# Block inverse on half the columns, and the scan's buffers moved so that the merge's first loads start inside its last chunks

## The chip, the cores and the metric

The kernel runs on one core of one Trainium2 chip. The metric is the device time of one execution in microseconds (us), taken as the median of the runs. All operands lie in HBM at the start, and the result is written back to it.

## The reference, cut to what matters

A residual block of width 1024 over 512 positions (and 256 positions of context) with three mixers side by side: an RWKV-7 scan, a convolution and a matrix LSTM. A gated merge, a projection and an MLP follow; then two layers of a second block, each with a feed-forward, a mixer made of a gated delta rule and two attentions, and another feed-forward. What the change touches is the RWKV scan, the delta rule and the merge:

```python
def step(S, inp):                      # RWKV-7, per position, 8 heads of 64, in both directions of time
    S = (S * w_t[:, :, None, :]
         - jnp.einsum('bhvk,bhk->bhv', S, kk_t)[..., None] * (kk_t * a_t)[:, :, None, :]
         + v_t[..., None] * k_t[:, :, None, :])
    y = jnp.einsum('bhvk,bhk->bhv', S, inp[5])

def _merge(u_gate, ya, yb, yc, pa, pb, pc, wo):
    ga, gb, gc = jnp.split(jax.nn.sigmoid(u_gate), N_BRANCH, axis=-1)
    m = ga * (ya @ pa) + gb * (yb @ pb) + gc * (yc @ pc)
    return m @ wo
```

`u_gate` is h @ w_in[:, OFF_GATE:], with h the normed input of the block. The delta rule of the second block has the same form of step.

## The kernel before, in words

**Engines and order.** Each engine has a program of its own, written out by hand in the order in which it runs (`tensor_program`, `vector_program`, `scalar_program`, `pool_program`, `sync_program`). An engine works strictly in that order and waits on semaphores: `K.at(name)` is the point at which a named result is done. `E.come(name)` marks how far an engine has got, `E.meet(name)` makes an engine wait for all marks of that name.

**Weights.** They come as slabs of 128x2048 fp32 (1 MB) into a ring of three slots, issued by the DMA queue of SP in `sync_program`. ACT copies a slab to a rounded form ("w hi", 128x2048), DVE subtracts to get the rest ("w lo"), and a product is three matmuls on the rounded parts (`mm3`, 128x512 each; one slab is 48 of them). `E.ahead()` is the place in the ACT and DVE programs at which the slabs up to the one after the current one are split, in order; `E.ahead_of(n)` splits up to the current slab plus n. `K.late[j]` names a mark that SP waits for before slab j is loaded.

**The scan** (`pe_rwkv` and its fellows). Time is cut into 6 tiles of 128 positions, each of two chunks of 64, for two directions d = 0, 1. Three streams per direction are interleaved in fixed turns by `rw_turns`: operands of a tile, the inverse of a tile, and the recurrence over the chunks; direction 1 runs five turns behind direction 0. The tile's triangular 64x64 blocks (8 heads, two chunks stacked on the partitions) are inverted by doubling, in `pe_invert`, `act_invert` and `dve_invert`: for n = 1 to 5 PE forms X = A T (16 matmuls 64x64, in fp32), ACT copies X to SBUF, PE forms the two products N of X with T and its transpose TT (32 matmuls; 16 for n = 5), and DVE takes over, with COPY_PREDICATED under the mask of level n, the half of the columns that this level changes (one instruction for TT, one for T, 128x512 each). In the profile an fp32 matmul is two records. There are 12 such inversions in the scan, and four per layer in the delta rule (`pe_prep`, `act_prep`, `dve_prep`, names `gd0`, `gd1`), so 8 there. Between the levels stands the rest of the scan's work on each engine. The first step (n = 0) works on 128x256 pieces (in the scan) or whole (in the delta rule).

**Memory.** The scan needs more room than the arena has: its buffers (`room` in `memory`) lie in the place of the block's input h (`m.hL`, spilled to `spill_h` before), in the ring of slabs, in a stretch of the arena from `mk2` on, and over part of the constants, all handed out in that order of places.

**From the scan to the merge.** After `E.meet("RWKV done")`, POOL (`pool_rw_out`) loads g2, two rows of norm parameters and h in two halves of 2 MB; SP loads slab 0 of the merge at once, and slabs 1 and 2 each after a half of h has landed (`K.merge_slab`). PE multiplies the gate by g2 (`pe_rw_out`, 4 fp32 matmuls 128x512), then takes slabs 0 and 1 (w_in for the first gate, with h), then slab 2 (p_c, with the split `yop`). DVE and ACT norm the scan's output in `dve_rw_out` and `act_rw_out`, with `E.ahead()` after the second of four tiles, and after the variance. ACT forms four sigmoids of the first gate, and then splits `ycT` to `yop`, which shares memory with what the norm reads, so that it waits for "rw out" 3, the end of the norm.

Of the kernel before, what the change touches and what calls it, by code (L numbers as in the profile page):

```python
# [17 lines left out]
SLOT = 2048  # L18
# [481 lines left out]
def sync_program(e, K):  # L500

    landed = [0] * NSLOT
    for j, (pieces, size, split) in enumerate(K.slabs):
# [3 lines left out]
        if j - K.merge_slab in (1, 2):  # L507
            e.wait_ge(*K.at("in", "hx", j - K.merge_slab - 1))
# [241 lines left out]
def memory(K):  # L750
# [89 lines left out]
    def room(n):  # L840
# [4 lines left out]
    m.Ya = m.ycT  # L845
    m.rsw = room(512)
    m.rw = [Names() for _ in range(2)]
    for d, s in enumerate(m.rw):
        s.SA, s.BK, s.UV = (room(1024) for _ in range(3))
        s.sets = [Names() for _ in range(2)]  # L850
        for z in s.sets:
            z.TK, z.MB, z.AK = (room(1024) for _ in range(3))
    for d, s in enumerate(m.rw):
        s.La, s.En, s.AT, s.T, s.X, s.Xs, s.St = (room(512) for _ in range(7))
        for z in s.sets:
            z.KKp, z.Rp, z.TT = (room(512) for _ in range(3))
            z.AT, z.T, z.X = s.AT, s.T, s.X
            z.edge = room(8)
        s.PCM = m.tmp[:, 512 * d:512 * d + 512]
# [1043 lines left out]
def pe_invert(t, K, st, s, key, ready):  # L1903

    for n in range(1, 6):
        o = t.take(st, "X", n, key)
        t.wait_ge(*(K.at(*ready) if n == 1 else K.at(st, "T", n - 1, key)))
        pe_blocks(t, (o, True, s.AT, s.T, (st, "X", n, key)))  # L1910
# [3 lines left out]
        both = [(o[0], False, s.X, s.TT, (st, "N", n, 0, key))]  # L1914
        if n < 5:
            both.append((o[1], True, s.TT, s.X, (st, "N", n, 1, key)))
        pe_blocks(t, *both)
# [3 lines left out]
def act_invert(a, K, st, s, key):  # L1921
# [14 lines left out]
def dve_invert(v, K, st, s, low, key):  # L1936
    for n in range(1, 6):
        m, mt = doubling(K, n, low)
        yield
        for j, (dst, msk) in enumerate([(s.TT, mt), (s.T, m)][:2 if n < 5 else 1]):  # L1940
# [2181 lines left out]
```

## Time and profile before

| | us |
|---|---|
| median of 3 runs (lowest to highest) | 4334.55 (4328.83 to 4341.07) |
| the profiled execution | 4335.74 |
| its span, first to last instruction | 4333.6 |
| mean granted clock of TensorE | 0.953 |
| PE busy | 4030.1 (93%) |
| DVE busy | 2159.5 (50%) |
| ACT busy | 1344.9 (31%) |

The stages that the change touches, in us from the span's start: the scan from about 530 to 966.6 (its last operands and inversions end near 935), the merge from 966.6 on, the delta rule of layer 0 from about 2180 to 2300 and of layer 1 from about 3504 to 3625. PE's clock is 1.0 at 2.4 GHz and 0.5 at 1.2 GHz. Busy shares are averages over stages with different limits, so each stage is read by itself. A matmul's record includes its way through the array: records overlap, and the spacing of a row of them is (time of the row less one record) / (count - 1).

### The profile page before, as it was taken

What the parts mean: (1) busy time and instruction counts of PE and PEld (TensorE: products, weight loads), DVE (VectorE), ACT (ScalarE), POOL (GpSimd) and SP (SyncE); (2) the same over time, 40 slices, a digit from 0 to 9 for tenths busy, and PEclk for the clock granted to TensorE, in tenths of its full rate; (3) what the DMA queues carried; (4) which work ended last, traced back from release to release, by engine and by line L of the source; (5) the groups of instructions that cost most, each with busy time, mean ns of one, the idle gap of its engine ahead of it and who ended that gap; (6) DMA issues with size and microseconds to landing.
All of it is one profiled execution on the core that took longest, in us unless ns stands there. A gap on an engine that the chain in (4) does not pass through costs nothing.

```text
span 4333.6 us, 70136 instructions
## 1 busy us (share of the span) xinstructions
PE 4030.1 (93%) x30330; PEld 3217.4 (74%) x30330; DVE 2159.5 (50%) x2941; ACT 1344.9 (31%) x1903; POOL 178.6 (4%) x214
## 2 busy tenths in 40 slices
PE   7998878888999999999988999999999988999998
PEld 5756768876767887888677578887888767578887
DVE  4866467754434445335665453345334755453335
ACT  4253233312324223222322532223222322433222
POOL 0000011211000000000010000000000001000000
PEclk9998879999999999999998899999999998999999
DMA  6212000004242223332102023332333101013331
GB/s 241 69 59 88 10 2 3 3 22 177 99 144 84 97 97 88 98 97 88 50 3 81 8 84 97 97 102 83 98 97 106 51 3 62 27 53 108 97 98 59
DMA packets 319781, 328.41 MB, mean 76 GB/s; under 512 B 10097, under 2 KB 243617, under 8 KB 318065
## 3 DMA queue, kind: packets, MB, share of 16 engines
q1 hardware_dynamic: 312144, 287.53, 21.4%
q0 software_dynamic: 7328, 36.40, 2.2%
q8 instruction: 239, 3.92, 0.4%
q14 instruction: 70, 0.57, 0.0%
HBM read 315.51 MB, written 8.39 MB: 75 GB/s over the span
## 4 chain that ended last, share of the span: by engine, by line
PE 80%; DVE 11%; ACT 4%; issue 3%; DMA 1%; POOL 0%; DVEq 0%; ACTq 0%; SPq 0%; POOLq 0%
PE psum L246 78%; DVE ring L300 2%; DVE ring L331 2%; DVE arena L300 2%; ACT ring L350 1%; PE psum L253 1%; ACT arena L350 1%; DVE arena L311 1%; DVE r L300 1%; ACT r L350 1%; DMA ring<-in_w_in 1%; DMA ring<-in_w_ada 0%; DVE arena L307 0%; DVE arena L331 0%; ACT L350 0%
## 5 line engine op out<-in xcount | busy, mean ns | idle before, releaser
L246 PE MATMUL psum<-r 128*128 128x512 f32 (+2 forms) x13008 | 2929.2, 387 | 68.9 <-DVE r L300 58.7
L246 PEld LDWEIGHTS psum<-r 128*128 128x128 f32 x13008 | 2369.7, 189 | 617.6 <-DVE r L300 53.0
L300 DVE TENSOR_TENSOR r<-ring,r 128x2048 fp32r<-128x2048 f32 (+2 forms) x261 | 575.7, 2206 | 385.3 <-ACT r L350 381.5
L350 ACT ACTIVATE r<-ring 128x2048 fp32r<-128x2048 f32 (+2 forms) x261 | 479.3, 1836 | 386.1 <-PE psum L246 325.7
L350 ACT ACTIVATE arena<-psum 128x512 f32<-128x512 f32 (+7 forms) x464 | 254.2, 548 | 1029.2 <-PE psum L246 949.0
L246 PE MATMUL psum<-arena 64*64 64x64 f32 (+15 forms) x2750 | 398.6, 318 | 39.9 <-DVE arena L300 23.1
L246 PE MATMUL psum<-ring 64*64 64x64 f32 (+4 forms) x8608 | 349.3, 234 | 82.3 <-ACT ring L350 35.6
L300 DVE TENSOR_TENSOR arena<-arena,psum 128x512 f32<-128x512 f32 (+4 forms) x224 | 132.6, 592 | 580.2 <-PE psum L246 560.9
L246 PEld LDWEIGHTS psum<-arena 64*64 64x64 f32 (+7 forms) x2750 | 252.4, 171 | 175.5 <-issue 118.1
L246 PEld LDWEIGHTS psum<-ring 64*64 64x64 f32 (+3 forms) x8608 | 287.4, 143 | 119.8 <-issue 46.7
L311 DVE SCALAR_TENSOR_TENSOR arena<-arena 128x512 f32<-128x512 f32 (+4 forms) x316 | 266.7, 844 | 117.9 <-ACT arena L350 106.8
L350 ACT ACTIVATE r<-arena 128x512 fp32r<-128x512 f32 (+1 forms) x176 | 109.4, 622 | 517.8 <-DVE arena L300 515.8
L350 ACT ACTIVATE ring<-psum 128x512 f32<-128x512 f32 (+5 forms) x262 | 140.4, 536 | 399.8 <-PE psum L246 330.0
L246 PE MATMUL psum<-ring,arena 64*64 64x64 f32 (+5 forms) x2408 | 195.8, 306 | 43.5 <-DVE ring L300 11.8
L300 DVE TENSOR_TENSOR arena<-arena 128x512 f32<-128x512 f32 (+6 forms) x298 | 183.2, 616 | 91.1 <-ACT arena L350 79.7
L246 PE MATMUL psum<-arena,ring 64*64 64x64 f32 (+4 forms) x2784 | 190.3, 258 | 16.9 <-ACT ring L350 7.1
L300 DVE TENSOR_TENSOR r<-arena,r 128x512 fp32r<-128x512 f32 (+1 forms) x176 | 119.8, 681 | 150.8 <-ACT r L350 148.1
L246 PEld LDWEIGHTS psum<-ring,arena 64*64 64x64 f32 (+4 forms) x2408 | 126.0, 150 | 88.9 <-issue 34.5
L246 PEld LDWEIGHTS psum<-arena,ring 64*64 64x64 f32 (+3 forms) x2784 | 153.0, 161 | 48.9 <-issue 30.6
L350 ACT ACTIVATE arena<-arena 128x512 f32<-128x512 f32 (+10 forms) x186 | 80.9, 435 | 334.2 <-DVE arena L307 158.3
L331 DVE COPY_PREDICATED ring<-arena,psum 128x512 f32<-128x512 uint32 (+1 forms) x202 | 136.1, 680 | 39.4 <-PE psum L246 29.9
L300 DVE TENSOR_TENSOR arena<-psum,arena 128x512 f32<-128x512 f32 (+5 forms) x107 | 70.4, 658 | 157.9 <-PE psum L246 97.5
(93 smaller groups left out, 1382.9 us busy)
## 6 DMA issues: line engine op xcount, KB each, us to landing
ring<-in_ffa_w_in SPq DMA_DIRECT2D x88, 512.0 KB, 5.1
ring<-in_ffb_w_in SPq DMA_DIRECT2D x88, 512.0 KB, 5.1
ring<-in_w_mlp SPq DMA_DIRECT2D x32, 1024.0 KB, 5.3
ring<-in_w_in SPq DMA_DIRECT2D x31, 1024.0 KB, 5.4
ring<-in_w_ada SPq DMA_DIRECT2D x24, 1024.0 KB, 5.4
ring<-in_mix_w_in SPq DMA_DIRECT2D x24, 1024.0 KB, 5.2
ring<-in_ffa_w_out SPq DMA_DIRECT2D x20, 1024.0 KB, 5.0
ring<-in_ffb_w_out SPq DMA_DIRECT2D x20, 1024.0 KB, 5.0
```

What stands on the lines that cost most here:

```text
L246: ins = self.raw.matmul(o, l, r, start=start, stop=stop, skip_group_check=True)
L253: ins = self.raw.transpose(o, i, self.K.C["ident"])
L300: self.done(self.raw and self.raw.tensor_tensor(o, a, b, f), keys)
L311: self.done(self.raw and self.raw.scalar_tensor_tensor(out=o, in0=a, scalar=s, in1=b, op0=f0, op1=f1), keys)
L331: self.done(self.raw and self.raw.copy_predicated(o, m, d), keys)
L350: self.done(self.raw and self.raw.activation(o, i, f, scale=scale, bias=bias), keys)
```

## The change

- **Inverse.** The products of level n are formed only for the columns that the level's mask can change: 32 of each 64, in pieces of 2^n columns (`some_columns`). Matmuls have the same stationary operand of 64x64 and 32 moving columns in place of 64; the results lie packed in 256 columns of a PSUM bank. ACT copies 128x256 to these columns of X, DVE's COPY_PREDICATED of n = 1 to 5 works on 128x256. X is set to zero once before the scan for each direction, and in the delta rule before the first tile of each stream. Counts of instructions stay.
- **Buffers.** `memory` puts into the places of h, of slots 1 and 2 of the ring and of g2 and the norm rows only what is not used in the last tile (position 5): the operand sets of even positions, BK, SA and La of direction 0.
- **Loads.** Inside the scan, at chunk 11 of direction 1, POOL marks "RWKV's first places free" and loads h, g2 and the rows (`pool_merge_loads`). Slabs 0 and 1 of the merge wait for this mark (ring position set so that they fall to slots 1 and 2), slab 2 for "RWKV done"; the waits of slabs 1 and 2 for the halves of h are gone. POOL's loads of `ycT`, `cv` and the constants move from the end of `pool_rw_out` to its start.
- **Splits.** `dve_rw_out` and `act_rw_out` split slab 0 first of all (`ahead_of(1)`), slab 1 after the four tiles in place of after the second, slab 2 after the variance as before.

```diff
 def sync_program(e, K):
-        if j - K.merge_slab in (1, 2):
-            e.wait_ge(*K.at("in", "hx", j - K.merge_slab - 1))
 def memory(K):
-    rooms = [[K.mem[1][:, mk_h - RING:mk_h - RING + 8192], 8192],
-             [K.mem[1][:, mk2 - RING:ARENA - RING], ARENA - mk2], [K.mem[0][:, 512:RING], RING - 512],
-             [lent, 128 * len(names) - m.cst_kept]]
+    early = [mem(mk_h, mk_h + 8192), mem(SLOT, 2 * SLOT), mem(2 * SLOT, 3 * SLOT), mem(mk2, mk2 + 1536)]
+    others = [mem(512, SLOT), mem(3 * SLOT, RING), mem(mk2 + 1536, ARENA), [lent, 128 * len(names) - m.cst_kept]]
+    for s in m.rw:
+        s.BK = room(1024, early)
+        for z, rooms in zip(s.sets, (early, others)):
+            z.TK, z.MB, z.AK = (room(1024, rooms) for _ in range(3))
...
 def dve_rw_first(E, K):
+    for x in m.rw:
+        v.set(x.X, 0.0)
+def some_columns(x, n, odd, heads=8):
+    b = 1 << n
+    head = [[64, heads]] if heads > 1 else []
+    return view(x[:, b * odd:], *head, [2 * b, 32 // b], [1, b])
+def pe_columns(t, n, *products):
+    for h in range(8):
+        for p in (0, 1):
+            for o, other, l, x, odd, key in products:
+                t.mm(o[HALF[1 - p if other else p], 32 * h:32 * h + 32], l[HALF[p], 64 * h:64 * h + 64],
+                     some_columns(x[HALF[p], 64 * h:], n, odd, 1), True, True, *([key] if h == 7 and p == 1 else []))
 def pe_invert
-        pe_blocks(t, (o, True, s.AT, s.T, (st, "X", n, key)))
+        pe_columns(t, n, (o, True, s.AT, s.T, odd, (st, "X", n, key)))
 def act_invert
-        a.copy(s.X, K.bank(st, "X", n, key), (st, "Xs", n, key))
+        a.copy(some_columns(s.X, n, 0 if low else 1), together(K.bank(st, "X", n, key), n), (st, "Xs", n, key))
 def dve_invert
-            v.cpred(h8(dst), msk, h8(K.bank(st, "N", n, j, key)), (st, "T", n, key))
+            v.cpred(some_columns(dst, n, c), m, together(K.bank(st, "N", n, j, key), n), (st, "T", n, key))
+def pool_merge_loads(E, K):
+    E.come("RWKV's first places free")
+    for half in range(2):
+        g.load(view(m.hflat[:, lo:], [4096, 2], [1, 2048]), ..., "hx", half)
+    g.load(m.g2f, K.I["rw_g2"][0], "g2f")
...
 def pool_rw_recur(E, K, d):
         g_.copy(s.UV[64:128, 512 * (c % 2):512 * (c % 2) + 512], m.vt[HALF[p], ti, :], (st, "v", c))
+        if (d, c) == (1, 11):
+            pool_merge_loads(E, K)
 def dve_rw_out(E, K):
+    E.ahead_of(1)
     for i in range(4):
...
-        if i == 1:
-            E.ahead()
     variance(3)
+    E.ahead()
 def tensor_program(E, K):
-    K.fences[E.slab] = K.late[E.slab] = "RWKV done"
-    K.merge_slab = E.slab
+    K.late[E.slab] = K.late[E.slab + 1] = "RWKV's first places free"
+    K.fences[E.slab] = K.late[E.slab + 2] = "RWKV done"
```

How the order moves, at three places. PE in the scan, at the first level of the first inverse: X and N are the 64x64 rows from ring to ring in the order before, and the 64x32 rows with the change; the 128x128 rows are operands of direction 1.

```order
L246 MATMUL psum<-ring 64x64 x16
L246 MATMUL psum<-arena 128x128 x4
L246 MATMUL psum<-arena,ring 128x128 x4
L246 MATMUL psum<-ring 64x64 x32
L253 MATMUL psum<-arena,ring 128x128 x8
```

```order
L246 MATMUL psum<-ring 64x32 x16
L246 MATMUL psum<-arena 128x128 x4
L246 MATMUL psum<-arena,ring 128x128 x4
L246 MATMUL psum<-ring 64x32 x32
L253 MATMUL psum<-arena 128x128 x8
```

As many matmuls stand there, at the same places; only the columns of the inverse's are halved.

POOL at the end of the scan: `r<-spill_h` is h, `in_rw_g`, `in_rw_lnb` and `in_rw_lnw` are g2 and the norm rows, the 64x512 copy is v of a chunk, the x12 row the work of `pool_rw_out`.

```order
+L375 COPY ring<-arena 64x512
+L386 DMA r<-spill_h 128x2x2048 x2
 L386 DMA arena<-in_rw_g 128x512
 L386 DMA arena<-in_rw_lnb 128x512
 L386 DMA arena<-in_rw_lnw 128x512
-L386 DMA r<-spill_h 128x2x2048 x2
-L371 TENSOR_TENSOR arena<-arena 128x512 x12
+L371 TENSOR_TENSOR arena<-arena 128x512
 L386 DMA arena<-spill 128x2048 x2
 L386 DMA arena<-in_consts 128x3200
+L371 TENSOR_TENSOR arena<-arena 128x512 x12
```

Five loads now stand ahead of the last product of the scan, which is the single L371 row; the three later loads stand ahead of the twelve operations.

DVE at the start of the merge, from the last row of the scan on, before the change and with it: L319 are sums, the `r<-ring,r 128x2048` rows are the "w lo" of a slab.

```order
L300 TENSOR_TENSOR arena<-arena,psum 64x512
L319 TENSOR_REDUCE arena<-arena 128x8
L305 TENSOR_SCALAR arena<-arena 128x8
L300 TENSOR_TENSOR arena<-arena 128x512
L319 TENSOR_REDUCE arena<-arena 128x8
L305 TENSOR_SCALAR arena<-arena 128x8
L300 TENSOR_TENSOR arena<-arena 128x512
L319 TENSOR_REDUCE arena<-arena 128x8
L300 TENSOR_TENSOR r<-ring,r 128x2048 x2
L319 TENSOR_REDUCE arena<-arena 128x8
L305 TENSOR_SCALAR arena<-arena 128x8
L300 TENSOR_TENSOR arena<-arena 128x512
```

```order
L300 TENSOR_TENSOR arena<-arena,psum 64x512
L300 TENSOR_TENSOR r<-ring,r 128x2048
L319 TENSOR_REDUCE arena<-arena 128x8
L305 TENSOR_SCALAR arena<-arena 128x8
L300 TENSOR_TENSOR arena<-arena 128x512
L319 TENSOR_REDUCE arena<-arena 128x8
L305 TENSOR_SCALAR arena<-arena 128x8
L300 TENSOR_TENSOR arena<-arena 128x512
L319 TENSOR_REDUCE arena<-arena 128x8 x2
L305 TENSOR_SCALAR arena<-arena 128x8
L300 TENSOR_TENSOR arena<-arena 128x512
L319 TENSOR_REDUCE arena<-arena 128x8 x2
```

In the order of the change one split comes ahead of the first tile, and none after the second; slab 1's follows after the last tile, ahead of the variance.

## Rows read from the trace of the kernel before

**Rows 1.** Page: the chain that ended last, by engine.
```profile
PE 80%; DVE 11%; ACT 4%; issue 3%; DMA 1%; POOL 0%; DVEq 0%; ACTq 0%; SPq 0%; POOLq 0%
```
**Rows 2.** Stretches: us, busy time (records) by engine, granted clock, DMA share, GB/s.
```profile
556.00:945.00 389.00, 335.21 (x8348) 313.73 (x8345) 266.47 (x405) 125.14 (x258) 67.68 (x85) 0.91 0.01 3
640.00:660.00 20.00, 16.93 (x305) 15.61 (x302) 8.76 (x13) 6.42 (x14) 0.00 (x0) 0.67 0.01 2
2170.00:2320.00 150.00, 117.52 (x3086) 101.23 (x3085) 90.59 (x141) 31.45 (x50) 21.05 (x16) 0.86 0.01 3
967.40:981.10 13.70, 6.03 (x8) 2.37 (x8) 6.26 (x8) 3.17 (x3) 8.98 (x9) 0.62 0.94 346
1014.70:1047.30 32.60, 32.60 (x133) 26.10 (x133) 11.47 (x10) 7.83 (x7) 0.00 (x0) 0.94 0.28 97
```
**Rows 3.** Chain by line, of the scan (556 to 945) and the delta rule (2180 to 2300).
```profile
by line: PE psum L246 50.7%; DVE ring L331 12.9%; DVE ring L300 8.6%; issue 7.5%; DVE arena L331 4.5%; DVE arena L307 2.9%; ACT ring L350 2.0%; DVE arena L300 1.8%; DVE arena L311 1.6%; PE psum L253 1.6%; DVE ring L327 1.6%; DVE ring L315 1
by line: PE psum L246 46.9%; DVE ring L300 16.2%; DVE ring L331 14.6%; issue 10.7%; DVE arena L300 6.4%; ACT ring L350 2.6%; DVE ring L315 1.2%; ACT L350 1.1%; DVEq L193 0.4%
```
**Rows 4.** Timeline of PE: products of the inverse, at full clock.
```profile
770.94 1.16 PE L246 MATMUL psum<-ring 64*64 64x64 f32 x64 [2.30 <-ACT ring L350]
818.08 1.15 PE L246 MATMUL psum<-ring 64*64 64x64 f32 x32 [0.33 <-DVE ring L331]
```
**Rows 5.** Timeline of PE: 128x128 stationary, few moving columns.
```profile
26.98 1.95 PE L246 MATMUL psum<-arena 66*128 66x2 f32 x16
2432.02 2.34 PE L246 MATMUL psum<-arena 128*128 128x64 f32 x20
```
**Rows 6.** Groups by form, 556 to 966: DVE's predicated copies.
```profile
L331 DVE COPY_PREDICATED ring<-arena,psum 128x512 f32<-128x512 uint32 x78 | 57.2, 734 | 8.2 <-PE psum L246 6.3
L331 DVE COPY_PREDICATED arena<-arena,psum 128x512 f32<-128x512 uint32 x30 | 22.1, 736 | 47.6 <-PE psum L246 47.0
L331 DVE COPY_PREDICATED ring<-arena,psum 128x256 f32<-128x256 uint32 x32 | 14.1, 441 | 1.8
```
**Rows 7.** Waits of PE in the scan (two rows), in the delta rule (one row).
```profile
PE psum L246 <- ACT ring L350: 26.2, 12, 3.6
PE psum L246 <- DVE ring L331: 14.2, 17, 4.5
PE psum L246 <- DVE ring L331: 6.2, 9, 1.8
```
**Rows 8.** Timeline of PE and POOL from the scan's end to the merge.
```profile
972.79 6.03 PE L246 MATMUL psum<-arena 128*128 128x512 f32 x8 [8.39 <-DMA arena<-in_rw_g]
981.17 24.09 PE L246 MATMUL psum<-r 128*128 128x512 f32 x96 [2.35 <-DMA r<-spill_h]
1014.68 32.78 PE L246 MATMUL psum<-r 128*128 128x512 f32 x132 [9.42 <-DVE r L300]
937.80 0.61 POOL L375 COPY ring<-arena 64x512 f32<-64x512 f32 x1
954.92 1.04 POOL L371 TENSOR_TENSOR arena<-arena 128x512 f32<-128x512 f32 x1 [16.52 <-DVE ring L300]
968.98 1.43 POOL L386 DMA_DIRECT2D r<-spill_h  x2
```
**Rows 9.** Timeline of DVE and ACT in the same stretch.
```profile
965.95 0.68 DVE L300 TENSOR_TENSOR arena<-arena,psum 64x512 f32<-64x512 f32 x1
977.22 3.15 DVE L300 TENSOR_TENSOR r<-ring,r 128x2048 fp32r<-128x2048 f32 x1 [6.43 <-ACT r L350]
990.60 2.29 DVE L300 TENSOR_TENSOR r<-ring,r 128x2048 fp32r<-128x2048 f32 x1 [10.23 <-ACT r L350]
988.65 1.92 ACT L350 ACTIVATE r<-ring 128x2048 fp32r<-128x2048 f32 x1 [11.46 <-DMA ring<-in_w_in]
1005.30 0.60 ACT L350 ACTIVATE arena<-psum 128x512 f32<-128x512 f32 x1 [0.52 <-PE psum L246]
1013.12 2.62 ACT L350 ACTIVATE r<-arena 128x512 fp32r<-128x512 f32 x4 [7.22 <-DVE arena L300]
```

More of the change, by code:

```diff
@@ L1900, in pe_blocks, with together, pe_invert @@
                      *([key] if h == 7 and p == 1 else []))
-def pe_invert(t, K, st, s, key, ready):
+def some_columns(x, n, odd, heads=8):
+    b = 1 << n
+    head = [[64, heads]] if heads > 1 else []
+    return view(x[:, b * odd:], *head, [2 * b, 32 // b], [1, b])
+def together(x, n):
+    b = 1 << n
+    return view(x, [32, 8], [b, 32 // b], [1, b])
+def pe_columns(t, n, *products):
[4 more added lines that the diff above has]
+                     some_columns(x[HALF[p], 64 * h:], n, odd, 1), True, True, *([key] if h == 7 and p == 1 else []))
+def pe_invert(t, K, st, s, low, key, ready):
+    odd = 0 if low else 1
     for n in range(1, 6):
@@ L1936, in dve_invert @@
 def dve_invert(v, K, st, s, low, key):
+    odd = 0 if low else 1
     for n in range(1, 6):
-        m, mt = doubling(K, n, low)
+        b = 1 << n
         yield
-        for j, (dst, msk) in enumerate([(s.TT, mt), (s.T, m)][:2 if n < 5 else 1]):
+        for j, dst in enumerate([s.TT, s.T][:2 if n < 5 else 1]):
             v.wait_ge(*K.at(st, "N", n, j, key))
@@ L1943, in dve_invert @@
                 v.wait_ge(*K.at(st, "N", n, 1, key))
[L1944 removed]
+            c = odd if j else 1 - odd
+            m = view(K.C[f"M{n}"][:, 64 * c + b * c:], [0, 8], [2 * b, 32 // b], [1, b]).bitcast(U32)
+            v.cpred(some_columns(dst, n, c), m, together(K.bank(st, "N", n, j, key), n), (st, "T", n, key))
             K.free(v, st, "N", n, j, key)
@@ L2167, in pe_rw_inverse @@
     for pos in range(6):
-        yield from pe_invert(t, K, f"rw{d}", K.m.rw[d].sets[pos % 2], pos, (f"rw{d}", "AT sb", pos))
+        yield from pe_invert(t, K, f"rw{d}", K.m.rw[d].sets[pos % 2], d == 0, pos, (f"rw{d}", "AT sb", pos))
 def act_rw_inverse(E, K, d):
@@ L2173, in act_rw_inverse @@
     for pos in range(6):
-        yield from act_invert(a, K, f"rw{d}", K.m.rw[d].sets[pos % 2], pos)
+        yield from act_invert(a, K, f"rw{d}", K.m.rw[d].sets[pos % 2], d == 0, pos)
 def dve_rw_inverse(E, K, d):
@@ L2249, in act_rw_recur @@
         yield
+def pool_merge_loads(E, K):
+    g, m = PoolLine(E, "rw"), K.m
+    E.come("RWKV's first places free")
+    for half in range(2):
+        lo = 2048 * half
+        g.load(view(m.hflat[:, lo:], [4096, 2], [1, 2048]),
+               K.I["spill_h"].rearrange("p (a b) -> p a b", a=2)[:, :, lo:lo + 2048], "hx", half)
+        for q in range(4 * half, 4 * half + 4):
+            K.points[("hx", "lo", q)] = K.points[("in", "hx", half)]
+    g.load(m.g2f, K.I["rw_g2"][0], "g2f")
+    g.load(m.lb, row(K.I["rw_lnb"][0, :], 512), "rw_lnb")
+    g.load(m.lw, row(K.I["rw_lnw"][0, :], 512), "rw_lnw")
 def pool_rw_recur(E, K, d):
@@ L2318, in pool_rw_out @@
     g, m = PoolLine(E, "rw"), K.m
-    g.load(m.g2f, K.I["rw_g2"][0], "g2f")
-    g.load(m.lb, row(K.I["rw_lnb"][0, :], 512), "rw_lnb")
-    g.load(m.lw, row(K.I["rw_lnw"][0, :], 512), "rw_lnw")
-    for half in range(2):
-        lo = 2048 * half
-        g.load(view(m.hflat[:, lo:], [4096, 2], [1, 2048]),
-               K.I["spill_h"].rearrange("p (a b) -> p a b", a=2)[:, :, lo:lo + 2048], "hx", half)
-        for q in range(4 * half, 4 * half + 4):
-            K.points[("hx", "lo", q)] = K.points[("in", "hx", half)]
+    g.load(m.ycB, K.I["spill"][:, 0:4, :], "ycT again")
+    g.load(m.cvT, K.I["spill"][:, 4:8, :], "cv again")
+    g.load(m.cst[:, m.cst_kept:], K.I["consts"][:, m.cst_kept:], "consts again")
     def added(i):
```

49 lines of the change are left out of this document (26 added, 23 removed).

## The prediction, made before the changed kernel was run

> **What bounds the kernel now.** I read the page first, then the stretches that the change touches. The chain that ended last is PE for 80% and DVE for 11% [rows 1]: shorter work elsewhere counts only where PE waits. The table of stretches [rows 2] is the second view: in the scan PE is busy 335 of 389 us, in the delta rule 118 of 150. The chain of these two stages alone [rows 3] is no longer PE's: about half of it is PE, and DVE's predicated copies (L331) are 17.4% of it in the scan (12.9 and 4.5), 14.6% in the delta rule. The third view is the timeline where the merge begins [rows 8, 9]. The scan ends with DVE's addition of y, at 965.95 + 0.68 = 966.63, here called T. PE then waits 8.39 us for g2, 2.35 more for h, and 9.42 before slab 2: between T and 1014.68 there are 48.05 us, of which PE works 30.12. DVE's row says why the last wait is there: its norm stood behind the splits of slabs 0 and 1, idle for 6.43 and for 10.23 us, the second until ACT had copied a slab that landed at 988.65.
>
> **Term 1: the start of the merge.** POOL issues the early loads after its copy that ends at 938.41 [rows 8]. The loads are 4 MB of h, 0.75 MB of g2 and rows, and SP's 2 MB of slabs 0 and 1, 6.9 MB in all. In the stretch in which the same transfers ran before, the engines moved 346 GB/s [rows 2]: 20 us, so that all has landed near 958.5, 8 us ahead of T. What is queued behind the five issues on POOL is one product of the scan, at 954.92; the same issues ended 3.8 us after T before (968.98 + 1.43), so they are done by 942.2 and hidden by over 12 us. SP has nothing else to issue there. The other loads that move on POOL, from the end of its work to T, come ahead of products that DVE needs some 20 us later: nothing.
>
> At T, PE starts with the gate: 6.03 us, then slabs 0 and 1 in 24.09 as before [rows 8], T + 30.1. The last sigmoid (0.60) and the step from ACT's first split to PE (1013.12 to 1014.68, 1.56) follow [rows 8, 9]: by PE's side slab 2 begins at T + 32.3. By DVE's side it is 48.05 less the two waits of 6.43 and 10.23, plus ACT's copy of slab 0 ahead of everything (1.92), plus a wait for slab 1's copy that DVE's last sum only half covers (1.2): T + 34.5. Of the 3.15 us that the split at 977.22 took, 0.9 goes if it runs like the one of 2.29 [rows 9]: T + 33.6. DVE is the later one, so slab 2 begins near T + 34: **14 us less** than 48.05. The low bound is 12.5, with POOL's work beside DVE slowing a little more of the norm; the high one is PE's side, 15.8, plus 2 if the granted clock, 0.94 in the 32.6 us after [rows 2], stays at 1.0 for want of the long wait: 18. Slab 0's split must be ready for PE at T + 6.03; it is at 1.92 + 2.29. Slab 1's must be at T + 18, and DVE gets to it after some 9.4 us of tiles: near T + 17.4, just in time. From slab 2 on PE is busy without a gap for 32.78 us [rows 8], so nothing gives the gain back.
>
> **Term 2: PE in the inverse.** Two products at full clock: 32 records on two quadrants (X) take 1.15 us, 64 on all four (N) 1.16 [rows 4]. Per quadrant both are 16 records, one behind the other: a record costs about 0.058 us (1.16 less 0.27 of the last record's way, by 15), be there two streams or four. In that time its quadrant loads 64 stationary columns and streams 64 moving ones twice. Which of the two sets it? The rows with a stationary operand of 128 columns answer [rows 5]: with 2 moving columns 16 records take 1.95 us, with 64 twenty take 2.34; less the last one's 0.27, 0.112 and 0.109 us each. Moving columns, from 2 to 64, change nothing; the loading does, and for half the stationary columns it scales to 0.056. That is what a record of the inverse costs now. The change halves the moving columns and not the stationary ones. So I take **0 us** for PE, the value of the nearest rows; the other bound is half the time, in the rivals. The Trainium skill has a rule that speaks against this part of the change: TensorEngine Tiling (Array Packing), section Instruction Overhead, says that a matmul with one moving column takes as long as one with 60. Rows 5 agree; by it the sum keeps the same 0 for the way from 64 to 32. Pieces of two columns (n = 1) are read in strides that no row shows; if they ran at half rate they would take what 64 columns took, so that costs nothing as well.
>
> **Term 3: DVE and ACT in the scan.** There are 12 x 9 = 108 copies of 128x512, 78 at 734 ns and 30 at 736; the same operation on 128x256 takes 441 ns [rows 6]. Each loses 0.293 us. The strided views could cost something; between 0.441 and 0.735 I take 0.441, the row of the same operation on the same count, which has pieces too. All 108 would be 31.6 us of DVE, but most lies beside PE's work. Above: the chain has 17.4% of 389 = 67.7 us of L331 [rows 3], of which the 44 small copies are at most 44 x 0.441 = 19.4; the rest is 48.3 us or 66 copies, 19.3 us. Below: PE waited 17 times for an L331 and 12 times for an ACT step that has one such copy ahead of it [rows 7]; 29 x 0.293 = 8.5. In the steady part PE is nearly full, and a faster DVE soon finds PE late instead, so I take **12 us**, nearer to the lower end. ACT's copies of X halve also; ring L350 is 2% of the chain [rows 3], and I leave it in the range. The two writes of zero ahead of the scan run while ACT and PE still form the first tanh: 0.
>
> **Term 4: the delta rule, per layer.** 36 of 44 copies get shorter. Above: 14.6% of 120 us is 17.5 us of L331 [rows 3], of it 36/44 halved, 14.3 us or 19.5 copies: 5.7 us. Below: 9 waits of PE [rows 7]: 2.6. DVE bounds much of this stage (PE idle 32 of 150 us [rows 2]), so the upper half applies: 4.5, for two layers **9 us**. Setting X to zero adds 0.5 us to DVE four times, while ACT works out an exponential for which it waits anyway.
>
> **Sum.** 14 + 12 + 9 = 35 us. The profiled execution took 4335.74 (span 4333.6 and 2.1 around it), 1.2 above the median of 4334.55: 4300.7 in its terms, 4299.5 in the median's. By the bounds the terms give 12.5 + 8.5 + 5.2 = 26 and 18 + 19.3 + 11.4 = 49: the likeliest case's own range is 4286 to 4309.
>
> **Rivals.**
> *A, the forecast:* PE's records keep their time, DVE gains, the merge starts early. 4300. For it: rows 5 and the timelines. Chance 0.72.
> *B, fewer moving columns do shorten a record.* For it: in rows 4 loading and streaming come to nearly the same time, so rows cannot tell them apart at 64 columns, and rows 5 are of full arrays, not of quadrants. 10 products per inversion by 0.43 us (16 records by 0.027), 120 in the scan and 80 in the delta rules: 86 us of PE, of which the share of PE in the chain passes, 50.7% of 52 and 46.9% of 34 [rows 3]: 42. 4258, and 4214 if all of it passes. The Trainium skill, TensorE: Matmul & The Clock Gate, section Back-to-back issue gap, gives a gap that falls with the moving columns, which would be this case; the same page's section on LDWEIGHTS gives 53 ns for 64 columns, which would be A. Chance 0.15.
> *C, the early start misses.* If the transfers run at half the rate beside the scan, they land after T by some 12 us and the first term falls to about 3; or the mark on POOL comes late. 4311. Against it: nearly no DMA in the scan now (share 0.01 [rows 2]). Chance 0.07.
> *D, the clock: slower than before.* With half the columns streamed in the inverse, TensorE does less, and its granted clock may fall. In the scan it is 0.91 over 389 us, and in 640 to 660, with PE busy for 85%, only 0.67 [rows 2]. A us of PE's work at 1.2 GHz in place of 2.4 costs half a us. To eat the 35 us it takes 70 us more at the low level, of some 630 in the three stages: the scan's mean would be at 0.82 or below. With 100 us more at that level it ends at 4300 + 50 = 4350. Against it: X, N and everything else are issued as densely as before. Chance 0.06, half of it beyond the point where it ends slower.
>
> **How the numbers follow.** The predicted time is A's, 4300. The range takes in A's own, C, the milder half of D and B down to 4250: 4250 to 4314, with about 2 in 10 outside. A measurement of this kernel tells about 0.3%, 13 us, from no change. Faster by over that: all of A and B and most of C, 0.91. Within: the rest of C and the middle of D, 0.06. Slower: 0.03.
>
> **What would show it.** In the profile after: h's DMAs start near 938 and PE has 96 matmuls within 7 us of the scan's end; the wait before the 132 matmuls is near 4 us, ended by DVE. Records 64x32 in runs of 64 still take some 1.1 us; if they take 0.7, it is B. COPY_PREDICATED of 128x256 near 441 ns, some 150 of them in the scan; PE's waits for L331 fall from 14.2 us to under 9. The granted clock of the scan is near 0.91; below 0.85 it is D. I am wrong on the sum if the scan gets more than 20 or less than 8 us shorter.

## The result, and the profile after

The changed kernel takes **4373.98 us** (median of 4 runs, 4367.93 to 4386.73) against 4337.22 of the kernel before beside it (4 runs, 4328.83 to 4341.07): ratio 1.0091, 95% interval 1.0064 to 1.0119. It is slower by some 37 us. The forecast was 4300, faster by over 0.3% with a chance of 0.91, in a range that ended at 4314: wrong in sign, and outside the range. Rival D, the clock, had "slower" at 0.03.

The profiled execution took 4386.73 us, the longest of the four, with a span of 4384.6 against 4333.6. A profile is one execution: this one is the longest of its four, and that of stream_all below the shortest of its four, so that their spans differ by 94 us where the medians differ by 73. Prices are therefore taken from medians, and profiles show where the time lies. First the page of the changed kernel: the chain by engine, then the slices of granted clock and the PE row.

```profile
PE   7998889998999999999988999999999988999998
...
PEclk9999856789999999999987899999999986999999
...
PE 84%; DVE 8%; ACT 4%; issue 2%; DMA 1%; POOL 0%; DVEq 0%; ACTq 0%; SPq 0%
```

DVE's part of the chain fell, 11% to 8% ([rows 1]), as it should have if the copies got shorter. PE's rose, 80% to 84%, though it issues as many matmuls. And the clock stands at 5, 6 and 7 tenths in the sixth to the eighth slice, which lie in the scan. Now stretches of the changed kernel (us, busy time and records of PE, PEld, DVE, ACT and POOL, granted clock, DMA share, GB/s): the whole scan, and the two delta rules from the last 128x512 product ahead of each to the first behind.

```profile
526.00:1010.00 484.00, 426.40 (x8608) 402.16 (x8606) 274.46 (x445) 127.69 (x289) 77.42 (x97) 0.73 0.05 17
2201.00:2351.00 150.00, 122.20 (x3044) 106.44 (x3043) 79.78 (x135) 24.54 (x44) 20.53 (x16) 0.74 0.01 3
3533.00:3692.00 159.00, 130.30 (x3041) 113.47 (x3038) 78.57 (x134) 24.23 (x44) 20.85 (x16) 0.70 0.01 3
```

The same three stretches of the kernel before, cut at the same instructions:

```profile
526.00:967.00 441.00, 362.92 (x8611) 338.21 (x8609) 293.88 (x449) 139.77 (x289) 72.56 (x92) 0.88 0.01 3
2174.00:2316.00 142.00, 109.52 (x3042) 94.11 (x3039) 86.13 (x132) 28.53 (x44) 21.05 (x16) 0.87 0.01 3
3499.00:3641.00 142.00, 109.23 (x3039) 94.19 (x3038) 86.04 (x132) 28.16 (x44) 21.04 (x16) 0.86 0.01 3
```

DVE works 19 us less in the scan and 6 to 7 less in each delta rule. PE works 63 us more in the scan, 13 and 21 more in the delta rules, with the same number of records. The granted clock is the only column that explains it: 0.88 to 0.73, 0.87 to 0.74, 0.86 to 0.70. With levels of 1.0 and 0.5, a mean c over w us is 2 (1 - c) w us at 1.2 GHz: 106 us of the scan before, 261 now.

The books of the two profiled executions: the scan ends at 1009.88 in place of 966.63 (+43.3), the delta rules get longer by 8 and 17 (+25), the merge starts 11.3 us earlier after the scan's end. That makes 57, of which the spans show 51; some 6 us lie elsewhere.

**PE's records.** Timeline of PE in the changed kernel, products of the inverse at either clock:

```profile
599.90 1.12 PE L246 MATMUL psum<-arena 64*64 64x32 f32 x32 [0.72 <-DVE arena L331]
622.31 1.92 PE L246 MATMUL psum<-ring 64*64 64x32 f32 x32
797.30 1.93 PE L246 MATMUL psum<-ring 64*64 64x32 f32 x64 [2.00 <-ACT arena L350]
3547.77 1.14 PE L246 MATMUL psum<-ring 64*64 64x32 f32 x64 [0.50 <-ACT ring L350]
```

At full clock 32 records take 1.12 us and 64 take 1.14, with 64 moving columns 1.15 and 1.16 ([rows 4]). So halving the moving columns left a product's time where it was, as forecast. At the low level the same 64 records take 1.93.

**DVE's copies.** Groups by form in the changed kernel, 552 to 1003:

```profile
L331 DVE COPY_PREDICATED arena<-arena,psum 128x256 f32<-128x256 uint32 x78 | 42.7, 548 | 73.3 <-PE psum L246 70.7
L331 DVE COPY_PREDICATED ring<-arena,psum 128x256 f32<-128x256 uint32 x74 | 35.5, 480 | 9.8 <-PE psum L246 7.8
```

The means are 548 and 480 ns, not the 441 of [rows 6]: this form has more than one duration, see the last section.

**The merge.** POOL, PE and DVE in the changed kernel from the mark in the scan to slab 2:

```profile
983.51 1.47 POOL L386 DMA_DIRECT2D r<-spill_h  x2
1010.12 5.37 PE L246 MATMUL psum<-arena 128*128 128x512 f32 x8 [2.47 <-issue]
1015.50 11.47 PE L246 MATMUL psum<-r 128*128 128x512 f32 x48
1030.10 11.46 PE L246 MATMUL psum<-r 128*128 128x512 f32 x48 [3.14 <-DVE r L300]
1046.61 33.65 PE L246 MATMUL psum<-r 128*128 128x512 f32 x132 [5.04 <-DVE r L300]
1012.16 3.28 DVE L300 TENSOR_TENSOR r<-ring,r 128x2048 fp32r<-128x2048 f32 x1 [2.28 <-ACT r L350]
1027.10 2.94 DVE L300 TENSOR_TENSOR r<-ring,r 128x2048 fp32r<-128x2048 f32 x1 [0.93 <-ACT r L350]
1033.14 2.29 DVE L300 TENSOR_TENSOR r<-ring,r 128x2048 fp32r<-128x2048 f32 x1 [2.10 <-ACT r L350]
```

The loads start 26 us ahead of the scan's end, and the waits of 8.39, 2.35 and 9.42 us ([rows 8]) are gone. From T = 1009.88, the end of DVE's last addition of the scan, to slab 2 are 36.7 us against 48.05. New are a wait of 3.14 before slab 1 and one of 5.04 before slab 2, both ended by DVE's split.

### The profile page after: what moved, and what is told of

The parts are those of the page before. It is cut to its first block, busy times and chain, and to the rows that moved or that the text cites. A ratio compares the mean times of both kernels' runs of the same rounds, so it can differ in the third digit from the quotient of the medians.

```text
span 4384.6 us, 70145 instructions
## 1 busy us (share of the span) xinstructions
PE 4119.1 (94%) x30330; PEld 3304.0 (75%) x30330; DVE 2131.2 (49%) x2947; ACT 1324.5 (30%) x1903; POOL 183.1 (4%) x214
## 3 DMA queue, kind: packets, MB, share of 16 engines
HBM read 315.51 MB, written 8.39 MB: 74 GB/s over the span
## 4 chain that ended last, share of the span: by engine, by line
PE 84%; DVE 8%; ACT 4%; issue 2%; DMA 1%; POOL 0%; DVEq 0%; ACTq 0%; SPq 0%
PE psum L246 82%; DVE arena L300 2%; PE psum L253 2%; ACT arena L350 1%; ACT ring L350 1%; DVE r L300 1%; ACT r L350 1%; DVE ring L300 1%; DVE arena L311 1%; DVE ring L331 1%; DMA ring<-in_w_ada 0%; DVE arena L331 0%; DMA ring<-in_w_in 0%; DVE ring L307 0%; ACT L350 0%
## 5 line engine op out<-in xcount | busy, mean ns | idle before, releaser
L350 ACT ACTIVATE arena<-psum 128x512 f32<-128x512 f32 (+6 forms) x506 | 267.9, 529 | 1125.0 <-PE psum L246 1031.5
L246 PE MATMUL psum<-arena 64*64 64x32 f32 (+11 forms) x6078 | 523.2, 286 | 52.6 <-DVE arena L300 23.1
L246 PEld LDWEIGHTS psum<-arena 64*64 64x64 f32 (+5 forms) x6078 | 358.9, 171 | 193.0 <-issue 115.3
L246 PE MATMUL psum<-ring 64*64 64x32 f32 (+5 forms) x7648 | 360.6, 258 | 49.6 <-ACT ring L350 12.9
L311 DVE SCALAR_TENSOR_TENSOR arena<-arena 128x512 f32<-128x512 f32 (+3 forms) x322 | 271.1, 842 | 117.9 <-ACT arena L350 106.8
L300 DVE TENSOR_TENSOR arena<-arena 128x512 f32<-128x512 f32 (+5 forms) x292 | 181.9, 623 | 91.6 <-ACT arena L350 79.7
L350 ACT ACTIVATE ring<-psum 128x256 f32<-128x256 f32 (+4 forms) x220 | 105.9, 482 | 368.6 <-PE psum L246 316.3
L246 PE MATMUL psum<-ring,arena 64*64 64x64 f32 (+6 forms) x1512 | 181.8, 372 | 34.5 <-DVE ring L300 10.4
L246 PE MATMUL psum<-arena,ring 64*64 64x64 f32 (+5 forms) x1312 | 137.7, 288 | 14.5 <-ACT ring L350 7.2
L246 PEld LDWEIGHTS psum<-arena,ring 64*64 64x64 f32 (+4 forms) x1312 | 105.7, 180 | 43.4 <-issue 29.5
```

What stands on the lines that cost most here:

```text
L246: ins = self.raw.matmul(o, l, r, start=start, stop=stop, skip_group_check=True)
L300: self.done(self.raw and self.raw.tensor_tensor(o, a, b, f), keys)
L311: self.done(self.raw and self.raw.scalar_tensor_tensor(out=o, in0=a, scalar=s, in1=b, op0=f0, op1=f1), keys)
L350: self.done(self.raw and self.raw.activation(o, i, f, scale=scale, bias=bias), keys)
```

## The experiments

Theory 1, formed on the stretches above: **the 32 moving columns lower TensorE's granted clock; everything else in the change pays about as forecast.** Its rivals: DVE's and ACT's shorter copies leave PE in another rhythm, and the clock falls with that; the moved buffers or loads slow PE; the reads in short pieces do; or the halved records are dearer by themselves. Each experiment's ratio is to the kernel before, run on the same chip beside it (4335.7 to 4337.5 us).

### PE's columns apart from the rest

**stream_all**: the changed kernel with PE's products whole again; DVE and ACT still take only 128x256 of them.

```diff
-        pe_columns(t, n, (o, True, s.AT, s.T, odd, (st, "X", n, key)))
+        pe_blocks(t, (o, True, s.AT, s.T, (st, "X", n, key)))
-        a.copy(some_columns(s.X, n, ...), together(K.bank(st, "X", n, key), n), ...)
+        a.copy(some_columns(s.X, n, ...), some_columns(K.bank(st, "X", n, key), n, ...), ...)
```

(and so for N and DVE's copies.) **old_inverse**: the changed kernel with the whole inverse of before. **half_only**: the kernel before with the changed inverse alone. **x_full**: X whole, N halved.

> The changed kernel, but PE streams all 64 columns in X and N again; ACT and DVE still work on 128x256, now picked out of a full bank of PSUM, and buffers, loads and splits stay as changed. Theory 1 (the granted clock fell because the inverse's matmuls stream half the columns): the scan's mean clock returns from 0.73 to 0.91 or more, X of 32 records takes 1.1 us nearly everywhere, and the time is that of my first forecast, 4300, within 10 us. Rival 2 (the clock fell because DVE and ACT are done sooner, or because buffers moved): the clock stays near 0.73 and the time near 4374. Rival 3 (strided pieces are read slowly by PE): the scan gets shorter, but with the clock unchanged.

> The changed kernel with the inverse of before whole (64 columns on PE, 128x512 on ACT and DVE, no setting to zero): what is left of the change is the placing of buffers, the early loads and the order of splits. Theory 1: clock of the scan 0.91, its length as before (about 437 us), and the start of the merge about 11 us shorter, as in the changed kernel: 4326. If the placing of buffers had slowed the scan (rival 2), it is 4350 or more.

> The kernel before with the inverse of the change only (32 moving columns, 128x256 on ACT and DVE), with buffers, loads and splits as before. Theory 1: the scan's clock near 0.73, the scan 47 us longer than before, the wait between scan and merge as before: 4385. If buffers or early loads were the cause, it is 4315 with a clock of 0.91.

> The changed kernel with 64 moving columns in X and 32 in N: a dose between the changed kernel and the one that streams all. Theory 1: the scan's mean clock lies between 0.73 and 0.91, nearer to 0.73 since N has the most matmuls (144 of 224 per inversion), and the time between 4300 and 4374, about 4345. Rival 2 (DVE and ACT done sooner): 4374 as in the changed kernel.

| kernel | PE's columns | DVE, ACT | buffers, loads, splits | us | ratio (95%) | scan's clock | clock of the whole, all executions |
|---|---|---|---|---|---|---|---|
| before | 64 | 128x512 | before | 4336.9 | 1 | 0.88 | 0.952 to 0.955 |
| old_inverse | 64 | 128x512 | changed | 4319.55 | 0.9962 (0.9947 to 0.9977) | 0.88 | 0.956 to 0.957 |
| stream_all | 64 | 128x256 | changed | 4300.60 | 0.9917 (0.9897 to 0.9938) | 0.88 | 0.955 to 0.959 |
| x_full | X 64, N 32 | 128x256 | changed | 4315.84 | 0.9943 (0.9927 to 0.9960) | 0.83 | 0.950 to 0.954 |
| changed | 32 | 128x256 | changed | 4373.98 | 1.0091 (1.0064 to 1.0119) | 0.73 | 0.928 to 0.933 |
| half_only | 32 | 128x256 | before | 4388.44 | 1.0118 (1.0099 to 1.0137) | 0.73 | 0.927 to 0.932 |

Stretches of stream_all, cut at the same instructions as above:

```profile
526.00:956.00 430.00, 362.29 (x8608) 338.49 (x8608) 273.63 (x445) 127.35 (x289) 78.41 (x97) 0.88 0.06 19
2148.00:2283.00 135.00, 105.11 (x3039) 92.05 (x3038) 78.34 (x134) 23.92 (x44) 20.88 (x16) 0.88 0.01 3
3465.00:3602.00 137.00, 106.52 (x3040) 91.10 (x3039) 79.33 (x134) 24.02 (x44) 20.86 (x16) 0.89 0.01 3
```

DVE and ACT are as short as in the changed kernel (274 and 127 us in the scan), the buffers and loads are the changed ones, and the clock is back at 0.88, PE's work at 362 us: the scan ends at 956.46 in place of 1009.88. The last column says the same of every execution, not only of the profiled ones: those of the two kernels with 32 columns are all at 0.933 or below, those with 64 at 0.952 or above. So neither DVE's rhythm nor the buffers did it. From the other side, half_only has neither the buffers nor the loads and loses the clock all the same. Between stream_all and the changed kernel lie 73 us by the medians, between old_inverse and stream_all 19, between before and old_inverse 17: the parts nearly add up, since half_only should be 73 - 19 = 54 above before and is 51.5.

Of the four expectations, stream_all's time (4300) and half_only's (4385, a scan 47 us longer) came out; old_inverse is 6 us faster than expected. The clock of 0.91 that stream_all was to return to was that of the stretch 556 to 945; over the whole scan the kernel before has 0.88 as well. x_full missed: some 4345 and a clock nearer to 0.73 were expected, for N has most of the matmuls, and it came to 4315.84 and 0.83. So the price is not in proportion to the number of matmuls that are halved.

### Stride, product, and the order of the splits

**contig** takes the same number of moving columns, but side by side (it leaves out the choice of columns, so the inverse holds other values):

```diff
-                     some_columns(x[HALF[p], 64 * h:], n, odd, 1), True, True,
+                     x[HALF[p], 64 * h + 32 * odd:64 * h + 32 * odd + 32], True, True,
```

**n_full** is x_full's other half: N whole, X halved. **best** is stream_all with slab 1 split after the third tile and slab 2's DVE half behind the norm:

```diff
         if i:
             variance(i - 1)
+        if i == 2:
+            E.ahead()
     variance(3)
-    E.ahead()
     v.ts(s[:, 0:32], s[:, 0:32], 1.0 / 64, 64e-5, MUL, ADD, ("rw n", "var"))
-    E.ahead()
...
         K.free(v, "rw gate", i)
+    E.ahead()
```

(and ACT's split of slab 1 after the third tile in the same way.) **order_before** is stream_all without `E.ahead_of(1)`, with `E.ahead()` after the second tile as before.

> The changed kernel, but each matmul of the inverse reads 32 moving columns that lie side by side, in place of the same number in pieces of 2 to 32 columns 64/2^n apart (it leaves out the right choice of columns, so the inverse holds other values; every count, wait and shape is the same). Theory 1 (the number of columns streamed sets TensorE's granted clock): nothing changes, 4374 us within 10, the scan's granted clock near 0.73, x32 products 1.12 us at full clock. Rival (reading in short pieces is what TensorE does badly, so that the lower clock or longer products come with the stride): the scan returns to 430 to 440 us with a clock near 0.88, and the time to 4300 to 4315.

> The changed kernel, N's products stream 64 columns again (144 of the 224 matmuls that an inversion issues), X's keep 32. With X whole and N halved the time was 4316 and the scan's clock 0.83. Theory 1, where the clock goes by the sum of the columns: 80 of 224 matmuls are halved instead of 144, so the scan's clock is above that, 0.85 to 0.87, and the time 4303 to 4313. Rival (the stretch that counts is the product with the fewest columns at a time: X issues 32 records on two quadrants, half of what N has in flight): the clock stays under 0.80 and the time is above 4330.

> The version in which PE streams 64 columns (4300.6 us, T to slab 2 36.7 us), with slab 1 split after the third of the norm's four tiles on DVE and ACT, not after the fourth, and DVE's half of slab 2 split behind the norm. Theory (PE's wait of 3.16 us before slab 1 and of 3.49 us before slab 2 are DVE's order): slab 1 is ready before PE, slab 2 begins 32 to 33 us after T, and the time is 4295 to 4298. Rival (slab 2's split is then late for PE in its turn, so the wait moves from slab 2's start to its second part or to the gated tiles): 4300 to 4304, no gain.

> The version in which PE streams 64 columns (4300.6 us), with the splits in the order of the kernel before: slab 0 only after two of the norm's four tiles, slab 1 after the fourth; loads and buffers as in the change. It prices the part 'the first slab split at once'. Theory: slab 0's split is ready some 7 to 9 us after T plus DVE's 2.3, so PE waits 2 to 5 us before slab 0 and slab 2 starts near T + 37 to 39: 4301 to 4304. Rival (slab 0's split is a gain of its own of over 8 us): 4309 or more.

**contig**: 4373.75 us, 1.0085 (1.0066 to 1.0105), clock 0.74 in its scan, 526 to 1008 (0.72 in 526 to 970, where the changed kernel has 0.71). As the changed kernel: the stride of the reads is not the cause. What is left is the 32 columns per matmul, and with them the packed place of the results in 256 columns of a bank, which contig keeps; no run has one without the other.

**n_full**: 4328.14 us (10 runs), 0.9977 (0.9964 to 0.9990), the scan's clock 0.79. Theory 1 as I had put it, that the clock goes by the number of halved matmuls, misses: it wanted 4303 to 4313. Halving the 80 matmuls of X costs 28 us against stream_all, halving the 144 of N 15, both 73; by the intervals each of these differences is known to some 10 us. X counts for more than its number. X issues 32 records on two quadrants in the time in which N issues 64 on four ([rows 4]), so its stretches are the sparsest; that was the rival's reason, and of its numbers the clock (under 0.80) was met and the time (above 4330) nearly. The reason itself is not shown, and the next section speaks against it. The price of both is more than the sum.

**best**: 4302.13 us, 0.9922 (0.9909 to 0.9935), no gain over stream_all. The timeline of PE at the start of the merge, in best (its T is 959.44) and in order_before (957.85):

```profile
959.65 5.37 PE L246 MATMUL psum<-arena 128*128 128x512 f32 x8 [2.44 <-issue]
965.06 11.47 PE L246 MATMUL psum<-r 128*128 128x512 f32 x48
976.78 11.46 PE L246 MATMUL psum<-r 128*128 128x512 f32 x48 [0.25 <-DVE r L300]
993.69 32.62 PE L246 MATMUL psum<-r 128*128 128x512 f32 x132 [5.46 <-DVE r L300]
```

```profile
958.05 5.37 PE L246 MATMUL psum<-arena 128*128 128x512 f32 x8 [2.44 <-issue]
967.45 24.21 PE L246 MATMUL psum<-r 128*128 128x512 f32 x96 [4.03 <-DVE r L300]
993.98 31.23 PE L246 MATMUL psum<-r 128*128 128x512 f32 x132 [2.31 <-DVE r L300]
```

The last two of the same rows in stream_all (T = 956.46):

```profile
976.70 13.01 PE L246 MATMUL psum<-r 128*128 128x512 f32 x48 [3.16 <-DVE r L300]
993.19 32.67 PE L246 MATMUL psum<-r 128*128 128x512 f32 x132 [3.49 <-DVE r L300]
```

In best slab 1 is no longer late (0.25 in place of 3.16), and PE waits longer before slab 2 (5.46 in place of 3.49): the theory's first half held, and the rival named what followed, 4300 to 4304. The start of slab 2 is T + 34.2, 2.5 us earlier than in stream_all, too little to show in the total. **order_before**: 4304.72 us, 0.9927 (0.9911 to 0.9942). PE waits 4.03 before slab 0, as expected, slab 2 starts at T + 36.1, and the time cannot be told from stream_all's. So DVE bounds this stretch in any order, and the third part of the change, slab 0's split at once, brings nothing that can be measured; what the merge gained comes, by subtraction, from the early loads and the buffers that make room for them.

### Can the clock be bought back with idle quadrants?

**x_twice** goes the other way from stream_all: X of levels 1 to 4 is also formed on the two quadrants that it leaves idle, into a bank that nobody reads. **x_twice_half** does the same to the changed kernel.

```diff
-        pe_blocks(t, (o, True, s.AT, s.T, (st, "X", n, key)))
+        pe_blocks(t, (o, True, s.AT, s.T, (st, "X", n, key)), *[(o2, False, s.AT, s.T, (st, "XX", n, key)) for o2 in more])
...
         a.wait_ge(*K.at(st, "X", n, key))
+        if n < 5:
+            a.wait_ge(*K.at(st, "XX", n, key))
```

> The version in which PE streams 64 columns (4300.6 us, the scan's clock 0.88), and in levels 1 to 4 of each inversion X is formed twice, the second time on the two quadrants that stand idle in it, into a bank of its own that nobody reads; ACT's copy waits for both. The change done the other way round: 64 more matmuls per inversion in time that is already spent (64 records on four quadrants took 1.16 us, 32 on two took 1.15). Theory 1 (the columns streamed at a time set the granted clock): the scan's clock rises above 0.88, to 0.93 or more, and the scan gets shorter by some 10 us: 4285 to 4295. Rival (more work cannot pay: 0.88 comes from the gaps in which PE waits, and the second bank makes PE wait for free banks): clock 0.88 or below, 4300 to 4320.

> The changed kernel (32 columns in X and in N, 4374 us, clock 0.73) with X formed twice in levels 1 to 4, on all four quadrants, in 32 columns each: the columns streamed per product of X are those of one whole X. X alone halved cost 28 us against the version that streams all, N alone halved 15, both together 73. Theory 1: the total per product counts, so this stands near the kernel in which only N is halved (4316, 0.83): 4315 to 4335, clock 0.80 to 0.84. Rival a (the moving columns of a single matmul count, however many quadrants run): nothing changes, 4365 to 4380, clock 0.73. Rival b (half matmuls tax PE in another way, such as more issues, and the clock is a companion): slower than 4380.

x_twice: 4346.52 us (9 runs), 1.0023 (1.0013 to 1.0033). x_twice_half: 4418.78, 1.0186 (1.0165 to 1.0208). Their scans and the steady part, 690 to 940:

```profile
526.00:978.00 452.00, 374.48 (x10143) 350.24 (x10142) 274.42 (x443) 127.44 (x289) 78.56 (x97) 0.86 0.05 19
690.00:940.00 250.00, 219.00 (x6499) 205.46 (x6491) 165.78 (x266) 68.27 (x155) 50.10 (x59) 0.95 0.01 4
```

```profile
526.00:1010.00 484.00, 411.46 (x10139) 387.16 (x10138) 275.70 (x443) 127.53 (x289) 78.82 (x97) 0.77 0.05 17
690.00:940.00 250.00, 223.38 (x5773) 210.82 (x5770) 153.92 (x243) 65.61 (x150) 48.19 (x56) 0.80 0.01 3
```

The same steady part of stream_all and of the changed kernel:

```profile
690.00:940.00 250.00, 226.50 (x5640) 212.32 (x5640) 166.43 (x269) 67.14 (x153) 55.13 (x67) 0.96 0.04 14
690.00:940.00 250.00, 232.64 (x4962) 219.43 (x4962) 153.20 (x243) 66.53 (x152) 47.85 (x56) 0.77 0.01 3
```

Both expectations of a gain fell. The rivals named the side: x_twice's had the clock (0.88 or below) but not the price (4300 to 4320), and x_twice_half is slower than 4380, as its rival b said. The work was not free: PE is busy for 12 us more in the scan of x_twice and idle for 10 more than in stream_all, and x_twice is 46 us above stream_all, x_twice_half 45 above the changed kernel. Half of the 46 lies outside the scan: in the profiles the scan is 22 us longer, the first delta rule 15 and the second 9.

Nor did it lift the clock in x_twice: 0.86 against stream_all's 0.88 in the scan, 0.95 against 0.96 in the steady part. For x_twice_half the profile alone would say otherwise, 0.77 against 0.73 in a scan of the same 484 us and 0.80 against 0.77 in the steady part; but its profile is of the shortest of its four executions and the changed kernel's of the longest. The clock of the whole execution over all of them, by medians, is 0.927 against 0.9325, and 0.954 against stream_all's 0.9565: a little lower both times. That the two prices are the same suggests that the second X cost 45 us by itself and that the half columns' 73 stayed whole; that reading is by subtraction, and what makes up the 45 (the second bank, ACT's wait for both, PE's own) was not taken apart. A gain through the clock that is smaller than these costs is not excluded.

### Two levels of five

**levels12**: the halved products in levels 1 and 2 alone, 96 of the 224 matmuls of an inversion.

```diff
+        if n < 3:
             pe_columns(t, n, (o, True, s.AT, s.T, odd, (st, "X", n, key)))
+        else:
+            pe_blocks(t, (o, True, s.AT, s.T, (st, "X", n, key)))
```

> The changed kernel with the halved products only in levels 1 and 2 of each inversion (96 of its 224 matmuls, X and N alike); levels 3 to 5 stream 64 columns. So far: none of 224 halved 4300.6 us and clock 0.88; the 80 of X 4328 and 0.79; the 144 of N 4316 and 0.83; all 224 4374 and 0.73. If the number halved set the clock, 96 would lie near 4315; the runs with X and N alone came out in the other order, so number alone does not tell. Theory 1a (the low level holds where X and N in succession are both short; a short product beside a whole one costs less than half of what two short ones cost): 3 of 7 of the products lie in such stretches, so 3 of 7 of 73 us: 4325 to 4338. Rival (X's products alone carry the price, whatever N does): 2 of 5 of X's 28 us plus at most as much: 4308 to 4320.

Measured 4318.28 us (5 runs), 0.9961 (0.9948 to 0.9975), the scan's clock 0.84. Theory 1a wanted 4325 to 4338 and is wrong; the count (4315) and the rival (4308 to 4320) both fit. Taking the prices as they stand, the runs give 18 us for 96 of both kinds, 15 for 144 of N, 28 for 80 of X, 73 for all 224: no single price per matmul fits them. That the matmuls with 32 moving columns lower the clock is shown; the law by which they do is open.

## Why the prediction was wrong, step by step

- **Term 2, the step that failed.** It says "So I take **0 us** for PE". Its ground, that a record's time does not fall with its moving columns, held: 1.12 and 1.14 us for the products. But the sum took the record's time at full clock for its cost, and put nothing for the level of the clock at which it would run. Measured, the halved columns cost 73 us by the medians (stream_all against the changed kernel), through the clock: 0.88 to 0.73 in the scan, 0.88 to 0.74 and 0.89 to 0.70 in the delta rules. The rule of the Trainium skill weighed there, TensorEngine Tiling (Array Packing), section Instruction Overhead, is that a matmul with one moving column takes as long as one with 60. The rows here agree with it, 1.12 us with 32 columns and 1.15 with 64; it is a rule on a matmul's own time, and the 73 us are not in that.
- **Rival D** had the mechanism and its place: "With half the columns streamed in the inverse, TensorE does less, and its granted clock may fall", with 100 us more at the low level ending at 4350; it came to more, 155 us in the scan alone, and 4374. What was wrong is its chance, 0.06, and its reason "X, N and everything else are issued as densely as before": dense issue did not hold the clock. [Rows 2] had warned of it, with 0.67 in a stretch in which PE was busy for 85%. At half a us each, with PE busy in 88% of the scan, the 155 us make 68 of PE's work; its row shows 63.
- **Term 1** said 14 us. The profile shows 11.3, the medians 17 (old_inverse against before, interval 10 to 23). The mechanism was right; the 2.7 us that the profile falls short are DVE's: its splits took 3.28 and 2.94 us where I had put 2.29, which is 1.6 of them, and the rest is mostly in its short instructions between (a TENSOR_SCALAR of 128x32 took 1.07 us, 0.50 before). These instructions ran beside POOL's twelve products, which now stand in one block at the start of the merge. POOL in the changed kernel, then before:

```profile
1012.22 7.53 POOL L371 TENSOR_TENSOR arena<-arena 128x512 f32<-128x512 f32 x4
1019.92 12.31 POOL L371 TENSOR_TENSOR arena<-arena 128x512 f32<-128x512 f32 x8 [0.17 <-POOL arena L371]
```

```profile
974.90 6.42 POOL L371 TENSOR_TENSOR arena<-arena 128x512 f32<-128x512 f32 x4 [4.49 <-DMA arena<-in_rw_lnb]
981.49 4.62 POOL L371 TENSOR_TENSOR arena<-arena 128x512 f32<-128x512 f32 x4 [0.17 <-POOL arena L371]
```

  The splits that overlap with them took 3.28 and 2.94 us (at 1012.16 and 1027.10) and 3.15 (at 977.22, before); those that do not took 2.29 (at 1033.14, and at 990.60 before). The prediction had this in its low bound, with POOL "slowing a little more of the norm", and the profile's 11.3 lies below its 12.5. No run moves POOL's work alone. PE's wait before slab 1, 3.14, is where I had called slab 1 just in time. The loads are also 4 + 0.75 + 2 = 6.75 MB, not the 6.9 of the text, and 2.2 of PE's 8.39 us of waiting lie before T; neither moves the term.
- **Term 3** said 12 us. Between old_inverse and stream_all the scan's end moves by 13.5, against the kernel before by 10.2: right in size. But not by the price put on a copy: "I take 0.441" was to take 31.6 us off DVE, and DVE's busy time in the scan fell by 19, since many of the copies took longer (548 and 480 ns in the mean). Most of what was missing will have lain beside PE's work, which no run shows; that the term came out so near is in part luck. PE's waits for L331 in ring, 14.2 us before ([rows 7]), were to be under 9; they are 8.6 in stream_all and 3.0 in the changed kernel, whose PE is the slower.
- **Term 4** said 4.5 us per layer. By the stretches above, before to stream_all, the delta rules went from 142 to 135 and from 142 to 137: 7 and 5, a little more than said. Terms 3 and 4 together were 21 us; by the medians of old_inverse and stream_all they are 19.
- **Terms 1, 3 and 4 together** were 35 us; stream_all, which has them without Term 2, is at 4300.6, by its ratio 27 to 45 below before. The forecast's number is that of another kernel.
- **Rival B** (shorter records) is excluded by the 1.12 and 1.14 us, and **rival C** (loads that miss) by the merge's rows.
- The list of what to look for worked: "The granted clock of the scan is near 0.91; below 0.85 is D". In 552 to 980 it is 0.73. So did "I am wrong on the sum if the scan gets more than 20 or less than 8 us shorter": it got 43 longer.

## What to carry to other kernels

Here halving the moving columns of 64x64 matmuls took nothing off their own time (1.15 to 1.12 us a product), and the granted clock of the whole stage fell for it, 0.88 to 0.73. Where the granted clock of a stage is below 1.0 already, price a cut in streamed columns through the clock first, and take the shorter copies on the other engines without it. In this case that is the version stream_all: PE streams all 64 columns, ACT and DVE read only the half that they need, and it beats the kernel before by 0.8% and the changed one by 1.7%. And when a chance is given to a mechanism whose price is larger than the whole gain, ask what row excludes it; "issued as densely as before" was not such a row.

## What the runs showed of the hardware that was not expected

- TensorE's granted clock in the scan went from 0.88 to 0.73 when each matmul of the inverse streamed 32 columns in place of 64, with as many matmuls, at the same places, and PE busy for 88% of the time in place of 84. The two cuts cost more together than one by one: X alone 28 us, N alone 15, both 73.
- Filling TensorE's idle quadrants in the products X did not raise the clock (0.86 with, 0.88 without), and cost 46 us.
- COPY_PREDICATED of 128x256 does not have one duration. The timeline of DVE in half_only, a copy at level 1, where the pieces are two columns wide, and a later one:

```profile
661.79 0.73 DVE L331 COPY_PREDICATED arena<-arena,psum 128x256 f32<-128x256 uint32 x1 [8.01 <-PE psum L246]
...
671.91 0.43 DVE L331 COPY_PREDICATED arena<-arena,psum 128x256 f32<-128x256 uint32 x1
```

  At level 1 half the columns take what all of them took (0.735 in [rows 6]), so that level gained nothing on DVE. In half_only these are the only long copies: of 156 copies in the scan 24 took 0.71 us or more, as many as level 1 has in 12 inversions, and the others 0.41 to 0.45. In the changed kernel and in stream_all, where the same operands lie elsewhere, 33 took 0.71 or more and another 38, all `arena<-arena,psum`, 0.46 to 0.61; so the placing of the buffers, or what it brings together in time, counts as well; which of the two is not shown.
